# Spreading the 128 gathered expert rows over two stages of a two-layer encoder: 64 and 64 before, 80 and 48 after

## The reference, cut to what matters

```python
    def block(args):
        xb, ib, gb = args                                # 128 tokens, their 128 expert indices, their gates
        a = jnp.einsum("td,ted->te", xb, u[ib])          # dot with the gathered up rows
        w = gb * jax.nn.gelu(a, approximate=False)
        return jnp.einsum("te,ted->td", w, v[ib])        # weighted sum of the gathered down rows
    return lax.map(block, (xt, it, gt)).reshape(bsz, seq, d)
```

## Time and profile before

| | |
|---|---|
| median of 3 runs | 4096.4 us |
| the profiled execution | 4095.8 us, its span 4093.7 us |
| TensorE busy | 3953.3 us, 97% of the span |
| VectorE busy | 2796.2 us, 68% |
| ScalarE, GpSimd busy | 1748.0 us (43%), 1153.4 us (28%) |
| the rows stage of the first layer | about 910 to 1509 us of the span |
| its block 1 | 1149 to 1318 us |
| the down stage of the first layer | 1509 to 2044 us |
| the same in the second layer | about 2940 to 3539, and 3539 to 4066 us |

### The profile page before, as it was taken

One profiled execution on the slowest core, in us unless ns is written; L12 is line 12 of the kernel. 1 busy time (PEld: TensorE's weight loads), 2 busy tenths in 40 slices (PEclk: granted clock), 3 DMA queues, 4 the chain that ended last, 5 costly groups with the idle time before them and its releaser, 6 DMA issues.

```text
span 4093.7 us, 59435 instructions
## 1 busy us (share of the span) xinstructions
PE 3953.3 (97%) x19746; PEld 3399.3 (83%) x19746; DVE 2796.2 (68%) x4541; ACT 1748.0 (43%) x3160; POOL 1153.4 (28%) x786
## 2 busy tenths in 40 slices
PE   7999999989999999999999999999899999999998
PEld 6677887789999988887866778877899999888886
DVE  2584351698887977777736843427988879677786
ACT  3533123225666654333346321322356666444343
POOL 1014563411211432222200155733011224222231
PEclk9999999999999999999999999999999999999999
DMA  3112332237877999999721122312478879999995
GB/s 125 48 64 81 104 104 70 95 106 249 297 283 280 392 375 345 347 347 343 275 77 48 62 92 103 119 57 89 152 245 291 289 281 405 371 345 349 347 357 183
DMA packets 360976, 879.48 MB, mean 215 GB/s; under 512 B 27856, under 2 KB 191952, under 8 KB 353872
## 3 DMA queue, kind: packets, MB, share of 16 engines
q1 hardware_dynamic: 153360, 508.21, 34.8%
q0 software_dynamic: 73728, 268.47, 17.2%
q10 hardware_dynamic: 133696, 100.67, 8.2%
HBM read 774.48 MB, written 102.76 MB: 214 GB/s over the span
## 4 chain that ended last, share of the span: by engine, by line
PE 77%; DVE 10%; DMA 3%; issue 3%; DVEq 2%; ACTq 2%; ACT 2%; POOL 0%; SPq 0%; POOLq 0%
PE ps L1223 44%; PE ps L1533 21%; PE ps L1510 3%; DMA raw<-in_experts 2%; PE ps L1236 1%; PE ps L1244 1%; ACTq L507 1%; PE ps L1285 1%; DVE wlo L807 1%; DVE acc L1092 1%; DVE ubuf L1085 1%; DMA act_e<-early_gelu 1%; PE ps L1303 1%; PE ps L1296 1%; PE ps L1295 1%
## 5 line engine op out<-in xcount | busy, mean ns | idle before, releaser
L1223 PE MATMUL ps<-xhi,whi 128*128 128x384 f32 (+1 forms) x3264 | 1189.7, 364 | 42.0 <-DVE inds L1070 14.0
L1223 PE MATMUL ps<-xlo,whi 128*128 128x384 f32 (+1 forms) x3264 | 1164.1, 357 | 0.0
L1223 PE MATMUL ps<-xhi,wlo 128*128 128x384 f32 (+1 forms) x3264 | 1164.1, 357 | 0.0
L476 ACT ACTIVATE whi<-raw 128x1024 fp32r<-128x1024 f32 x666 | 698.3, 1054 | 362.8 <-PE ps L1533 268.9
L807 DVE TENSOR_TENSOR wlo<-raw,whi 128x1024 fp32r<-128x1024 f32 x512 | 622.2, 1218 | 161.0 <-ACT whi L476 156.9
L1223 PEld LDWEIGHTS ps<-xhi,whi 128*128 128x128 f32 x3264 | 618.0, 189 | 100.2 <-issue 36.8
L1223 PEld LDWEIGHTS ps<-xlo,whi 128*128 128x128 f32 x3264 | 618.1, 189 | 51.0 <-issue 5.3
L1223 PEld LDWEIGHTS ps<-xhi,wlo 128*128 128x128 f32 x3264 | 616.9, 189 | 48.9
L1533 PE MATMUL ps<-whi,eh 128*128 128x512 f32 x1536 | 601.6, 392 | 26.3 <-DVE el L1184 26.1
L436 POOL DMA_INDIRECT ubuf<-in_up_rows,gidx x256 | 290.6, 1135 | 1100.6 <-DVE small L1085 913.2
L1533 PE MATMUL ps<-whi,el 128*128 128x512 f32 x1536 | 599.8, 391 | 0.0
(11 more groups left out here) (216 smaller groups left out, 4879.3 us busy)
## 6 DMA issues: line engine op xcount, KB each, us to landing
raw<-in_experts SPq DMA_DIRECT2D x512, 512.0 KB, 6.4
raw<-in_back SPq DMA_DIRECT2D x112, 512.0 KB, 3.2
gate_table<-gbuf SPq DMA_DIRECT2D x48, 1024.0 KB, 6.6
act_e<-early_gelu ACTq DMA_DIRECT2D x128, 384.0 KB, 7.2
gtile<-gate_table ACTq DMA_DIRECT2D x30, 1536.0 KB, 23.3
raw<-in_front SPq DMA_DIRECT2D x64, 512.0 KB, 3.2
raw<-in_gates SPq DMA_DIRECT2D x48, 512.0 KB, 3.2
early_gelu<-weighted SPq DMA_DIRECT2D x128, 192.0 KB, 5.2
```

Source lines behind the costliest of these rows:

```text
L476: A(whi[:, SLOT[s]:SLOT[s] + 1024], raw[:, SLOT[s]:SLOT[s] + 1024], ACT.Copy).then_inc(rounded[s], 1)
L1223: ins = MM(out, w[:, a:a + P], x[:, c, t0:], start=(i == 0 and n == 0), stop=(i == len(chunks) - 1 and n == 2))
```

## The change

The middle block takes two selections in a half group, so that 16 × (1 + 2 + 2) = 80 are done in the rows stage and 48 in the down stage. In the down stage these are 12 in 16 steps: three steps of four have one and the fourth has none. VectorE and ScalarE get that spread from the formulas they already have; GpSimd's list of counts had been one per step and is now written out as `late`.

```diff
-SELS_OF = (1, 1, 2)
+SELS_OF = (1, 2, 2)
 SEL_EARLY = sum(SELS_OF) * HALVES
...
+                late = [SELS * (r + 1) // STEPS - SELS * r // STEPS for r in range(STEPS)] * (PAIRS // STEPS)
                 old = range(0)
-                for count in [n for n in SELS_OF for _ in range(HALVES)] + [(SEL - SEL_EARLY) // PAIRS] * PAIRS + [0]:
+                for count in [n for n in SELS_OF for _ in range(HALVES)] + late + [0]:
```

## The result

The changed kernel takes 4145.55 us (median of 4 runs, 4143.22 to 4148.78), the kernel before 4095.83 us in the same comparison. The ratio is 1.012, with a 95% interval of 1.0104 to 1.0136: slower, as forecast, by 50 us where 51 were forecast from the profiled execution.

A forecast was written before the change was run, and what follows sets the result against it. TensorE, busy 97% of the span, was taken as the bound, with VectorE becoming the bound of block 1 after the change. 4095.8 + 2 × 27.5 − 4 = 4146.8, about 4147 us, 1.2% slower; range 4127 to 4170.

The forecast's parts named there:

- The pace of block 1: Block 1: VectorE's half group goes from 9.09 to 11.7 us, 1.6 us over TensorE's 10.10, so VectorE becomes the bound.
- VectorE's arrival at the end of the picks: Block 1: 40.1 us of added dots and axpys less 4.5 us of lost waits, so VectorE gets there 35.6 us later.
- The crossing: From block 1's last pick to block 2's first one-hots: 14.5 us instead of 22.6, so block 2 starts 27.5 us later.
- Transfers in block 1: Block 1: 16.8 MB come in, making 347 GB/s, under the 389 of block 2, so transfers stay behind VectorE.
- rival on late gathers: Block 1: gathers take longer than their buffers give, VectorE waits on line 1085, 26 us more, 4173; chance 2%.
- a rule of the Trainium skill: GpSimd's gathers: transfers can starve for descriptors while VectorE holds the shared port pair; the trace showed landings within 10 us.
- rival on transfers: Block 1: transfers bind it as well, full DMA engines costing some 10 us as in block 2, 4167; chance 7%.
- The clock: Block 1: rival that TensorE's granted clock falls with its idle time, 12.2 us a half group, 16 us, 4163; chance 4%.
- Block 2: Block 2: same instructions, order and buffers, its transfers bounding its second half as before; taken at nothing.
- The down stage, the term of the wrong size: Down stage: fewer selections give back at most TensorE's 8.1 us of waits for `el`; half taken, 4 us for both layers.

The follow-up runs named there:

- the other direction: One selection a half group in all three blocks (48 in the rows stage, 80 in the down stage), against the kernel before; ratio 1.0203, 4181.95 us.
- 24, 20 and 20: The kernel before, still 64 and 64, with its rows-stage selections placed 24, 20 and 20 in the three blocks instead of 16, 16 and 32; ratio 0.9988.
- early transpose: The kernel before, with the transpose of the next block's picks moved ahead of the crossing pair on TensorE, its copy likewise on ScalarE; ratio 0.9983.
- VectorE alone: The kernel before with block 1's 16 dots and 15 of its 16 axpys made twice, no transfer or coefficient added; ratio 1.0125.

## Why the prediction was right, point by point

- **The pace of block 1.** 11.73 us measured, 11.7 forecast, and the mechanism (VectorE the bound, TensorE waiting for the second panel's low part) is shown by the chain: the picks or the added work removed, the loss is gone; the work alone added, it is back.
- **VectorE's arrival at the end of the picks.** It took 1331.66 − 1146.84 = 184.8 us instead of 148.3: 36.5 late, 35.6 forecast.
- **The crossing.** 13.4 us instead of the 14.5 worked out, since ScalarE loaded the exponential's table while it waited for the picks; VectorE's idle time there was 7.2 us, forecast 7. Together the block lost 27.4 us, forecast 27.5.
- **Transfers in block 1.** 331 GB/s measured over the block and its crossing, 347 forecast without it. That they do not bind is shown with the picks left out, at 386 GB/s. The rival on late gathers falls too: VectorE waited for none. The prediction set the trace against a rule of the Trainium skill (page "SBUF — State Buffer", section "SBUF: two separate sides"), but that section ties late descriptors to VectorE instructions in a two-port mode, such as an fp32 copy within SBUF. It does not say that the dots, one-hots and axpys here would make gathers late, so this trace neither bears it out nor goes against it.
- **The price of the rival on transfers was misread.** The pair that ends at 1491.75 is the crossing one. The last one-hot matmuls of block 2 end at 1481.63 + 1.78 = 1483.41, so its 16 half groups took 163.1 us and not 171.4. With 16 or 20 selections in block 2 (the other direction; 24, 20 and 20) they take 160.0. Full DMA engines cost block 2 some 3 us and not 10, and that rival should have stood at about 4153.
- **The clock.** The granted clock stayed 1.00, its level of 2.4 GHz, in block 1 with TensorE idle 22 of 198 us. That rival falls.
- **Block 2.** I took nothing; it became 1.9 us longer in both layers. The kernels with 32 selections there, a loaded block 0 or 1 and no early transpose have 187.8 to 191.8 us, around the 188.8 and 188.0 of before. The size is small and its cause stays open.
- **The down stage, the term of the wrong size.** I took 4 us and called 8.1 the most, from TensorE's waits in the earlier trace rows. The profiles show 13.0. Over the four profiled kernels with 64 selections there and without other changes to the stage (before, VectorE alone, 24-20-20, early transpose) the stage takes 527 to 534 us, mean 530; in all with 48 it takes 523.4 to 525.0. So 6 us a layer come back, 12 in all, and the bound was wrong. A mended term would have given 4139, still within the range.
- **Why the bound was wrong.** The listed waits count from the modelled end of the matmul before. From start to start two down matmuls are 0.227 us apart; all that is over this in the two down stages adds up to 16.0 us before and 3.1 after, a difference of 12.9, which is the whole gain. The 8.1 us of listed waits are 10.7 counted so, with two of about 0.1 us that the list leaves out. Another 1.6 us is the clock: right after the longest wait, 2.2 us at 1919.6, the granted clock was 0.50 for 3.4 us (first row: us, busy time of PE, PEld, DVE, ACT and POOL, granted clock, DMA share, GB/s).

```profile
1919.60:1922.80 3.20, 3.19 (x8) 2.52 (x9) 3.04 (x3) 1.31 (x2) 0.15 (x1) 0.50 0.91 312
```

- **Behind `el` stood ScalarE and a transfer.** I read these waits as VectorE's, as the list names `el`. The chain goes further back. At five of the six waits of the first layer it leads to ScalarE, which stood 10.6 to 11.8 us in the issue of its own load of Gelu rows (line 507), and before the sixth to a landing of such rows, 20.5 us. The rows at the longest wait follow; the next issue took 0.39 us:

```profile
1902.60 12.65 ACTq L507 DMA_DIRECT2D act_e<-early_gelu  x1
1915.36 0.20 ACT L717 ACTIVATE small<-small 128x1 f32<-128x1 f32 x1 [11.92 <-issue]
...
1915.92 0.39 ACTq L507 DMA_DIRECT2D act_e<-early_gelu  x1
...
1918.59 0.96 DVE L1184 TENSOR_TENSOR el<-weighted,eh 128x768 fp32r<-128x768 f32 x1 [0.45 <-ACT eh L769]
1919.61 0.79 PE L1533 MATMUL ps<-whi,eh 128*128 128x512 f32 x1 [2.22 <-DVE el L1184]
```

  In the down stage of the first layer ScalarE's idle time of this kind was 118.3 us in 13 waits; with 48 selections it is 26.3 in 8:

```profile
ACT small L717 <- issue: 118.3, 13, 11.9
```

```profile
ACT whi L477 <- issue: 26.3, 8, 4.7
```

  So what the selections gave back there probably came through ScalarE's queue of loads rather than through VectorE's time. No run takes only the gathers or only VectorE's work out of that stage, so which of the two frees the queue stays open.
- **Luck in the sum.** The down stage gave back 9 us more than I took. Block 2's 3.8 us and the 5.1 us that untouched code took more in this profile, together 8.9, hid that error. That the forecast came within 2 us is luck; the 27.5 us of block 1 are not.

## What to carry to other kernels

Before work is moved beside a bound engine, read how fast the other engine goes in a stretch where it waits for nothing (here 9.09 us against 10.10), and add the new work from start to start: what counts is the spare time in that block, not the engine's 68% of the span. The idle time that a block can give is a sum of its own (pace, head start, crossing); up to it selections were nearly free, past it they cost their full price. Where the last bit of spare time lies in a hand-over between blocks, moving one small instruction ahead of a long one frees it. Here the same 80 and 48 went from 1.2% slower to 0.3% slower by spreading the selections over two blocks, to 0.6% slower by the early transpose, and to 0.4% faster by both. And a wait is best followed past the engine that the list names, and counted from start to start.

## What the runs showed of the hardware that I had not expected

The DMA engines served block 1 at 386 GB/s and a share of 0.98 with TensorE unhindered (171.1 us against 170.9), while in block 2 at 389 GB/s and 0.99 they cost only some 3 us. A share near 1 did not by itself tell a stage that transfers bound.

The issue of a load on ScalarE, mostly a matter of 0.4 us, held that engine for 12.65 us at the longest wait of the down stage before, and ScalarE's idle time of this kind came to 118.3 us there.

A table load on ScalarE ran while the instruction behind it still waited for its semaphore: in the crossing after the change it ran from 1330.92 to 1332.20 us, and the gaps that the exponential needs were ready only at 1332.20. That took 1 us off the crossing.
